# Both MLPs of a two-layer trunk by Strassen's seven block products, with the whole up projection ahead of the down projection

## The reference, cut to what matters

```
def sq_relu_mlp(h, w_up, w_down):
    u = jax.nn.relu(h @ w_up)          # (1024 x 1024) @ (1024 x 4096)
    return (u * u) @ w_down            # (1024 x 4096) @ (4096 x 1024)

def reference(x, ...):
    x = x + diff_attention(rms_norm(x, attn_norm_g[0]), ...)
    x = x + sq_relu_mlp(rms_norm(x, mlp_norm_g[0]), mlp_w_up[0], mlp_w_down[0])
    k_sh, v_sh = shared_kv(x, kv_norm_g, w_kv, kv_k_norm_g)
    x = x + swa_sink_attention(rms_norm(x, attn_norm_g[1]), ..., k_sh, v_sh)
    x = x + sq_relu_mlp(rms_norm(x, mlp_norm_g[1]), mlp_w_up[1], mlp_w_down[1])
    return x
```

## Time and profile before

| | us |
|---|---|
| median of 3 runs (lowest to highest) | 2523.49 (2523.09 to 2526.92) |
| span of the profiled execution | 2514.6 |
| PE busy | 2393.3 (95%) |
| DVE, ACT, POOL busy | 1158.5, 847.4, 777.5 |

### The profile page before, as it was taken

The page is one execution under the profiler, slowest core; times in us unless marked ns, Lnnn a source line. Parts: engine busy times, 40 slices in busy tenths (PEclk is TensorE's granted clock), DMA queues, the critical chain, the costliest instruction groups (busy, mean ns, idle before and its releaser), DMA issues.

```text
span 2514.6 us, 38441 instructions
## 1 busy us (share of the span) xinstructions
PE 2393.3 (95%) x12652; PEld 2057.0 (82%) x12652; DVE 1158.5 (46%) x2385; ACT 847.4 (34%) x1892; POOL 777.5 (31%) x1429
## 2 busy tenths in 40 slices
PE   6999999977999999999999889988999999999999
PEld 5888888866888888888888888887888888888887
DVE  5677777775424222222235368885434222222321
ACT  4455555543222121131132256653331131220221
POOL 2333333352222312213225255552222213223222
PEclk9999999978999999999999999998999999999999
DMA  6001000012111111111113110003111111111122
GB/s 185 26 26 27 25 25 26 1 51 59 50 51 50 42 50 50 45 47 50 50 50 101 42 35 19 0 26 101 50 47 46 50 50 49 42 50 50 47 60 69
DMA packets 205069, 120.92 MB, mean 48 GB/s; under 512 B 11424, under 2 KB 197792, under 8 KB 204960
## 3 DMA queue, kind: packets, MB, share of 16 engines
q1 hardware_dynamic: 194208, 111.19, 15.2%
q10 hardware_dynamic: 10752, 8.39, 1.0%
HBM read 106.98 MB, written 12.58 MB: 48 GB/s over the span
## 4 chain that ended last, share of the span: by engine, by line
PE 81%; DVE 8%; issue 5%; ACT 3%; POOLq 1%; DVEq 1%; POOL 0%; DMA 0%; ACTq 0%
PE score L1373 64%; PE proj L1373 10%; PE pv L1373 5%; ACT p L775 1%; DVE p L1090 1%; PE trb L1628 1%; PE trb L1411 1%; DVE p L1112 1%; DVE r L1237 1%; DVE wa_lo L1005 1%; DVE pb L1320 1%; ACT pb L970 0%; DVE wT_lo L1005 0%; DVE wb_lo L1006 0%; DVE coef_a L1107 0%
## 5 line engine op out<-in xcount | busy, mean ns | idle before, releaser
L1373 PE MATMUL score<-a_hi,w_hi 128*128 128x512 f32 x1152 | 449.7, 390 | 4.5 <-DVE w_lo L1005 4.5
L1373 PE MATMUL score<-b_hi,w_hi 128*128 128x512 f32 x1152 | 450.1, 391 | 2.5 <-DVE w_lo L1005 2.5
L1373 PE MATMUL score<-b_lo,w_hi 128*128 128x512 f32 x1152 | 448.7, 390 | 0.0
L1373 PE MATMUL score<-a_lo,w_hi 128*128 128x512 f32 x1152 | 448.7, 389 | 0.0
L1373 PE MATMUL score<-b_hi,w_lo 128*128 128x512 f32 x1152 | 366.9, 389 | 0.0
L1373 PE MATMUL score<-a_hi,w_lo 128*128 128x512 f32 x1152 | 366.7, 389 | 0.0
L651 POOL TENSOR_TENSOR xT<-xT,e 128x512 f32 (+1 forms) x112 | 189.5, 1714 | 408.8 <-DVE e L1217 408.8
L724 ACT ACTIVATE w_hi<-w_raw 128x1024 fp32r<-128x1024 f32 x144 | 151.5, 1052 | 476.5 <-PE score L1373 472.5
L639 POOL TENSOR_TENSOR e<-e 128x512 f32<-128x512 f32 x128 | 134.6, 1059 | 548.2 <-ACT e L869 547.2
L1217 DVE TENSOR_TENSOR e<-score,r 128x512 f32<-128x512 f32 x128 | 84.1, 688 | 423.1 <-PE score L1373 423.1
L1373 PEld LDWEIGHTS score<-a_hi,w_hi 128*128 128x128 f32 x1152 | 216.8, 188 | 50.6 <-DVE w_lo L1005 5.4
(11 more groups left out here) (245 smaller groups left out, 4140.4 us busy)
## 6 DMA issues: line engine op xcount, KB each, us to landing
w_raw<-in_mlp_w_up SPq DMA_DIRECT2D x64, 512.0 KB, 4.0
w_raw<-in_mlp_w_down SPq DMA_DIRECT2D x64, 512.0 KB, 3.7
wa_raw<-in_a_w_qkv SPq DMA_DIRECT2D x96, 128.0 KB, 2.4
xT<-xT_dram SPq DMA_DIRECT2D x16, 512.0 KB, 3.6
x_tok<-in_x SPq DMA_DIRECT2D x8, 512.0 KB, 6.8
xT_dram<-x_stage SPq DMA_DIRECT2D x16, 256.0 KB, 2.6
w_raw<-in_a_w_o SPq DMA_DIRECT2D x8, 512.0 KB, 4.3
xT_dram<-xT ACTq DMA_DIRECT2D x16, 256.0 KB, 2.0
```

The costliest lines, as they stand in the source:

```text
L1373: return nc.tensor.matmul(out, a, b, start=start, stop=stop, **kw)
```

## The change

Both MLPs are computed by the form of Strassen's scheme with seven products and shared sums. The 2x2 blocks of a product are: of the weights, even and odd k-chunks by even and odd output chunks of 128 columns; of the activations, even and odd k-chunks by the two halves of tokens. One "pair" n is 256 output columns. It takes seven operands of weights (A11, A12, A22 and the sums S1 to S4), seven "slots" of activations (three blocks, the sums T1, T2, T4 and one more) and seven products. A product is 4 k-pairs x 3 = 12 matmuls of 128x512. There are 32 pairs to an MLP (16 of up, then 4 slices of 4 of down), so 224 products and 2688 matmuls; before, the MLP had 64 panels and 3072. `wo` is as before, in 8 panels.

What else is new:

- POOL makes four sums of weights to a pair (`sum_weights`), each 128x512; ACT and DVE split each of the seven weight operands by itself (`op_of_weights`, 128x512), DVE 4 products ahead (`LEAD`), ACT 5.
- S2, S3 and A22 of a pair go into the same bank as A11, and S4 into that of S1, on top of what stands there. So ACT copies the bank out after A11, after S2, after S3 and after A22 (`up_read`), and a product waits until the copy in front of it is made (`wait_bank`). In down DVE adds the bank to `xT` each time (`down_add`).
- After up, for each pair, DVE adds the products from the other banks (`up_add`, 3), ACT applies ReLU (3 more than the one in the last read) and squares (4), DVE multiplies by `r2` (`up_scale`, 4) and makes the sums for the way down (`up_sums`, 4), all on 128x512 in a buffer `quad`. SP stores the seven tiles (1.75 MB) in the new `u_dram`.
- All of up runs first. The operands of activations `xop01`, `xop23` hold 4 k-pairs by 7 slots by hi and lo. Before each of the four down slices they are refilled: 14 loads of 512 KB from `u_dram` into staging buffers, each split by ACT (`refill_hi`) and DVE (`refill_lo`) as 128x1024. Slice 0 has two staging buffers, later ones have a third (`ss`). The table of steps (`refill_at`) gives one refill to a product over 14 products, and slot j of a slice is refilled between its last use in one slice and its first in the next.
- The factor `r2` is needed ahead of the squares' way to DRAM, so the reciprocals stand in DVE's steps 5 and 6 of up (`factor`).
- `x` comes in for `wo` in pairs of chunks (`load_unit`), its sums with `wo` are parked in DRAM half by half, and come back in `xT` when `quad` is no longer needed (`load_xT`). DVE starts the weight splits of the second `wo` panel without waiting for `x`.
- At the end of down there is no POOL addition any more; output DMAs are issued by SP.
- The places in SBUF of most tiles are new; all loops over panels are unrolled.

The steps of the three engines are numbered by product: in its step k an engine handles what follows product k-1.

```diff
+def product(n, kind):
+
+    if kind == "A11":
+        return 7 * n - 2 if n else 0
+    at = {"S1": 1, "S2": 2, "A12": 3, "S3": 4, "A22": 6, "S4": 7}[kind]
+    return 7 * n + at - (1 if n == NP - 1 and at > 4 else 0)
...
+def refill_at(k):
+
+    found = []
+    for s in range(SLICES):
+        last = 7 * (NU + 4 * s - 1)
+        for h in range(14):
+            step = last - 1 + h if h < 2 else last + h
+            if step == k:
+                found.append((s, h))
+    return found
...
+                def load_refill(s, h):
+                    b, before = refill_buffer(s, h)
+                    if h == 0:
+                        for i in range(2):
+                            sp.wait_ge(u_stored[i], 16 * (NU // 2 * seg + 2 * s + 2))
...
+                    elif s or h >= 2:
+                        behind = 2 if s == 0 or (s == 1 and h < 2) else 3
+                        sp.wait_ge(op_split, refill_splits(seg, s, h) - behind)
...
+                    if k == 7 * NU + 1:
+                        sp.wait_ge(u_stored[0], 16 * (NU // 2) * (seg + 1))
+                        for c in range(1, 4):
+                            load_xT(c)
...
+                def up_read(n, m):
+
+                    act.wait_ge(prod, products(seg, n, ("A11", "S2", "S3", "A22")[m]))
...
+                def refill_hi(s, h):
+                    b, before = refill_buffer(s, h)
+                    slot, v = divmod(h, 2)
+                    act.wait_ge(prod, products(seg, NU + 4 * s - 1, KIND_OF_SLOT[slot]))
+                    act.wait_ge(st_in[b], 16 * (refills_of[b] * seg + before + 1))
+                    copy((xop01, xop23)[v][:, slot, :, 0, :], st[b][:, :, :]).then_inc(op_hi, 1)
...
+                        if 0 <= n < NU:
+                            if at in (1, 3, 5, 7):
+                                up_read(n, at // 2)
+                            if at in (5, 7, 8):
+                                up_relu(n, (5, 7, 8).index(at))
+                            for m, when in enumerate((6, 8, 8, 9)):
+                                if at == when:
+                                    up_square(n, m)
...
+                def factor(half):
+
+                    cols = slice(HALF * half, HALF * (half + 1))
+                    dve.wait_ge(ss_sum, 3 * seg + half + 1)
+                    nc.vector.tensor_scalar(r2[:, cols], (proj, pv)[half][:, :], 1.0 / D, EPS, ALU.mult, ALU.add)
+                    dve.drain()
+                    nc.vector.reciprocal(r2[:, cols], r2[:, cols])
...
+                    if k + LEAD < OPS:
+                        op_of_weights(k + LEAD)
+                    if k in (5, 6):
+                        factor(k - 5)
+                    for s, h in refill_at(k):
+                        refill_lo(s, h)
...
+                    elif n < NU:
+                        if kind == "S4":
+                            pe.wait_ge(u_added, 3 * NU * seg + 3 * n + 2)
+                        else:
+                            pe.wait_ge(u_copied, 4 * NU * seg + 4 * n + {"S2": 1, "S3": 2, "A22": 3}[kind])
...
+                    if n >= NU and n % 4 == 0:
+                        pe.wait_ge(op_split, refill_splits(seg, (n - NU) // 4, 2 * slot + 1))
```

1020 lines of the change are left out of this document (650 added, 370 removed).

## The result

The changed kernel takes 2478.49 us (median of 4 runs, 2476.03 to 2479.33), the kernel before 2523.38 (4 runs, 2523.09 to 2526.92). The ratio is 0.9816, 95% interval 0.9802 to 0.9830: 45 us faster. The forecast was 2403, range 2352 to 2462: the sign is right, and 75 us of the gain are missing.

A forecast was written before the change was run, and what follows sets the result against it. PE was taken to bound the kernel, time following the number of matmuls. Span 2514.6 - 174.1 removed + 62.4 given back - 7.0 = 2395.9, with 8.9 between span and median 2404.8; given as 2403, range 2352 to 2462.

The forecast's parts named there:

- What bounds the kernel, and what is removed: MLPs: PE-bound, 0.2267 us per matmul; 768 fewer matmuls take off 174.1 us; 12 in a row into one bank cost nothing.
- The way up: Up, step 8 of each pair: PE stalls 0.4 us on ACT's chain and bank read, 6.4 us per MLP.
- Start of up: First pair of each MLP: PE waits for the chain with the two reciprocals, 3.8 us, plus 1 for the first weight sum.
- The 1 us for the first weight sum: Start of up: POOL makes the first weight sum behind the squares of the last wo chunk, 1 us per MLP.
- Refills: Down slices: refills fall behind PE, 11 us in slice 0 and 3 in each later slice, 20 per MLP; bounds 5 and 45.
- the ring: Staging buffers of the refills: they set the pace once a load takes over 4.6 us in slice 0, 6.35 later.
- The lock: Refills: DVE stands still while POOL works, counted as 0.7 of POOL's 8.3 us, 5.8 us.
- DMA elsewhere: wo stages: segment 1's second panel no longer waits for x, -2.1 us; the chain at segment 0's start loses about 0.5.
- The clock: Gaps of PE also cost clock, 0.69 and 0.89 us round two earlier gaps; used only in a bound.
- Exit of segment 0: End of segment 0: PE's stand of 6.35 us shrinks to 2.5 us in all, -3.9.
- Late refills: Rival, refills: slow loads in one SP stream make the kernel slower than before, from a landing of 8.6 us; chance 0.03.
- Locked out: Rival, refills: POOL's whole time adds to DVE's, 20 us, and S2 and S3 wait, 34: 2457; chance 0.18.

The follow-up runs named there:

- e1: Changed kernel with ScalarE reading the next pair's first bank ahead of the last ReLU and two squares of the pair before; 2452.8 us.
- e8: Changed kernel with SyncE issuing the refill load ahead of the weight pair in steps that have both; 2441.4 us.
- e12: e8 with GpSimd's weight sums cut to 8 of 128 columns, leaving out part of the computation; 2424.8 us.
- e5: Changed kernel with the third wo panel's load issued right behind the first two, ahead of x and the first weight pair; 2472.5 us.
- Four edits of order: Changed kernel with refill ahead of weight pair, bank read first, second factor later and third wo panel's load first, all together; 2414.3 us.

## Why the prediction was wrong

- **What bounds the kernel, and what is removed: right.** PE, 0.2267 us per matmul, 174.1 us off. The new order of banks costs nothing.
- **The way up: right in mechanism and place, a little small.** Forecast 0.4 us per pair from ScalarE's step-8 chain, measured a wait of 0.41 behind ScalarE's read and a pair of 19.73 us for 19.04, 0.69 in all. Some 0.15 of the difference is that a row's idle time is that much shorter than the gap in the spacing; the rest is in the matmuls behind it. e1 takes it all away.
- **Start of up: a step left out.** I let PE wait for the factors once, at the end of the chain. The addition of step 6 stands in that chain, behind the first factor, and S4 waits for it: 2.5 us in MLP 0 and 3.9 in MLP 1, then 4.1 and 1.3 for the end of the chain, 6.6 and 5.2 for 3.8 forecast. And ScalarE's first bank read, 1.85 us late behind its splits and squares, was not in the sum. The 1 us for the first weight sum does not show as a wait of its own.
- **Refills: the step that failed.** I put the load at 3.6 us, the median of xT's loads in the earlier trace rows, and let the ring bind from a mean landing of 4.6 or 6.35. The median of the 84 loads into `st` came out at 4.7 and the mean of all 112 at 5.0, which by my own formula costs under 3 us per MLP. But a refill that has one step of slack does not see a mean. The last one in each slice stands behind a weight pair in the same queue and lands after 6.6 to 8.2 us. I had the queue in the prediction ("one SP stream") and priced only its average. Forecast 20 us per MLP, measured 29.9 and 29.5, and with their low clock 38.5 and 38.6; the order of two loads accounts for 37 us of both MLPs (e8).
- **The lock: right in kind and about right in size.** I counted seven tenths of POOL's 8.3 us in each slice. In the sum that is all of the 3 us of each later slice and up to 5.8 of slice 0's 11, about 15 per MLP and 30 in all. Cutting the sums gives 29 us; once the refill goes ahead of the weight pair it gives 17 (e8 to e12).
- **DMA elsewhere: wrong by one load.** I took 0.5 us off at segment 0's `wo`. The third panel's load moved behind ten loads of x and a weight pair: +4.8 (e5 gives the queue's 3.6 back). In segment 1 the w_lo wait went as forecast (-2.1), and the same late load put 2.3 and its low clock in its place.
- **The clock: not in the sum.** It stood only in a bound of the earlier trace rows. It costs 25.6 us in the two MLPs; it follows 13 of their 16 waits of 2 us or more.
- **Exit of segment 0: the wait shrank as forecast, 6.35 to 2.08, but not the time.** The matmuls behind it wait again:

```profile
1374.06 0.36 PE L1728 MATMUL pv<-wb_hi,b_hi 128*128 128x256 f32 x1 [2.08 <-issue]
1375.42 0.58 PE L1728 MATMUL pv<-wb_hi,b_hi 128*128 128x256 f32 x1 [0.78 <-DVE wb_lo L1274]
1376.84 0.58 PE L1728 MATMUL pv<-wb_hi,b_hi 128*128 128x256 f32 x1 [0.40 <-DVE wb_lo L1274]
1380.71 0.55 PE L1728 MATMUL pv<-wb_hi,b_hi 128*128 128x256 f32 x1 [0.95 <-DVE b_lo L1273]
```

  By the 72nd matmul, attention B is 1.2 us behind the kernel before; another 3.5 us are low clock in the 250 us after. With one trace of before I can't say whether those belong to the change.
- **The rivals.** Late refills got 3% and was asked to decide at a mean landing of 8.6; its mechanism, in the tail and not in the mean, is half of what was missed. Locked out (2457) is the nearest number, but not by its mechanism: it adds 20 us to a lock that was already sized right, and 34 for many small waits of S2 and S3, where the traces show few and long ones. The range was too narrow because the bounds of the refills (5 to 45 per MLP) were in the sum, while the range was cut from the middle of the cases.

The miss of 82 us of span (forecast -118.7, measured -37.2) is so: MLPs 59, of which 26 low clock, 19 the refills' waits, 8 the start's and 4 the way up's; `wo` 9; attention and the end 13. About 7 of the 82 are the short execution in the trace of before, which is why the medians miss by only 75; most of the attention's part no edit explains.

## What to carry to other kernels

Where loads share a queue, what counts for a load with a step of slack is what is issued just ahead of it and not its median landing: list for each late-needed load what stands before it, and put it ahead of loads with more slack. Do the same for an engine's program: a read that PE waits for goes ahead of work with a deadline a step later. And count with a wait of PE the low clock that can follow it: here 1.1 to 2.8 us, behind two in three of the waits of 2 to 3.6 us and behind all longer ones. Four edits of order gave this kernel more (64 us) than the change itself had (45).
